# Values and gate columns from seven products a tile pair, dilated values put in slot order through DRAM

## The reference, cut to what matters

```
proj = h @ w_in
q_n, kv_n, gate_n, qkv_d, merge = jnp.split(proj, IN_SPLITS, axis=-1)
...
gate_n = jax.nn.sigmoid(gate_n)                       # 24 columns
kv_n   -> NSA keys and values: compressed, selected, window
qkv_d  -> 3 dilation groups x 4 heads x 64: q, k, v
...
for g, (window, d) in enumerate(DIL_PAIRS):           # d = 1, 4, 16
    # sub(): token t of the sequence goes to subsequence t % d
    o, lse = banded_attention(sub(q[:, :, g]), sub(k[:, :, g]), sub(v[:, :, g]), window // d, ...)
```

## Time and profile before

| | |
|---|---|
| time, median of 3 runs | 1754.91 us (1751.19 to 1756.32) |
| the profiled execution, its own time | 1753.52 us |
| its span (first to last instruction) | 1751.6 us |
| busy: PE, PE weight load, DVE, ACT, POOL | 1628.7, 1069.8, 646.8, 406.9, 176.3 us |
| mean granted TensorE clock | 0.98 of full speed |

### The profile page before, as it was taken

How to read it: one execution, slowest core, us unless ns; L and a number is a source line. 1 busy time by engine, 2 the same in 40 slices (tenths; PEclk the granted TensorE clock), 3 DMA queues, 4 the chain that set the end, 5 groups by cost and what they waited for, 6 DMA issues and landing times. The chain is left out here.

```text
span 1751.6 us, 37114 instructions
## 1 busy us (share of the span) xinstructions
PE 1628.7 (93%) x16025; PEld 1069.8 (61%) x16025; DVE 646.8 (37%) x1594; ACT 406.9 (23%) x908; POOL 176.3 (10%) x220
## 2 busy tenths in 40 slices
PE   5999999999999998999999999999999999998783
PEld 3444445898777786644444445556777767666562
DVE  3533332001767666766655455561000000000003
ACT  4000000001666666610010003221121122111112
POOL 1205000000111110000000000001111111111100
PEclk9999999999999999999999999989999999999996
DMA  9874224131011107334452172169999999999996
GB/s 341 258 230 112 74 84 146 37 104 42 2 44 44 33 2 237 111 111 129 120 145 83 37 280 85 68 258 390 391 383 384 394 387 382 396 392 397 406 385 229
DMA packets 146623, 356.07 MB, mean 203 GB/s; under 512 B 14751, under 2 KB 94231, under 8 KB 121851
## 3 DMA queue, kind: packets, MB, share of 16 engines
q1 hardware_dynamic: 120656, 305.50, 47.0%
q0 software_dynamic: 12656, 28.01, 6.0%
q10 hardware_dynamic: 13148, 20.18, 3.3%
HBM read 320.53 MB, written 45.36 MB: 209 GB/s over the span
## 5 line engine op out<-in xcount | busy, mean ns | idle before, releaser
L2635 PE MATMUL psum<-sb_m_xT,sb_m_ring 128*64 128x64 f32 (+2 forms) x4096 | 152.0, 235 | 22.0 <-issue 17.7
L2635 PEld LDWEIGHTS psum<-sb_m_xT,sb_m_ring 128*64 128x64 f32 x4096 | 147.8, 140 | 35.6 <-issue 34.7
L2384 ACT ACTIVATE sb_m_xT<-psum,sb_rowmod 128x64 f32<-128x64 f32 (+2 forms) x256 | 81.7, 424 | 216.3 <-PE psum L2623 216.3
L2519 DVE TENSOR_TENSOR sb_m_hT<-psum,sb_m_sg 128x256 f32<-128x256 f32 (+2 forms) x32 | 15.3, 477 | 308.9 <-PE psum L2635 308.9
L748 PE MATMUL psum<-sb_vD,sb_room 128*128 128x512 f32 x240 | 104.7, 593 | 0.2 <-DVE sb_vD L685 0.2
L2635 PE MATMUL psum<-sb_m_xT,sb_front 128*64 128x64 f32 (+2 forms) x2560 | 94.5, 236 | 9.9 <-issue 7.3
L2635 PEld LDWEIGHTS psum<-sb_m_xT,sb_front 128*64 128x64 f32 x2560 | 92.4, 142 | 17.2 <-issue 16.9
L1008 ACT ACTIVATE sb_d_probs<-sb_d_probs,sb_d_nmax 128x640 f32<-128x640 f32 (+7 forms) x128 | 92.9, 735 | 1.6 <-DVE sb_d_nmax L1048 1.0
L2642 PE MATMUL psum<-sb_m_ring,sb_m_hT 128*64 128x512 f32 (+2 forms) x256 | 84.5, 611 | 5.6 <-DMA sb_m_ring<-in_exp_w_dram 4.7
L780 PE MATMUL psum<-sb_b_wvd,sb_rows 128*128 128x256 f32 x384 | 88.9, 394 | 0.0
L780 PEld LDWEIGHTS psum<-sb_b_wvd,sb_rows 128*128 128x128 f32 x384 | 84.9, 286 | 3.3
(11 more groups left out here) (384 smaller groups left out, 2408.8 us busy)
## 6 DMA issues: line engine op xcount, KB each, us to landing
sb_m_ring<-in_exp_w_dram SPq DMA_DIRECT2D x48, 2048.0 KB, 34.4
sb_front<-in_exp_w_dram SPq DMA_DIRECT2D x30, 2048.0 KB, 33.8
sb_rows<-in_exp_w_dram SPq DMA_DIRECT2D x18, 2048.0 KB, 36.5
sb_g_ada<-in_ada_w_dram SPq DMA_DIRECT2D x16, 1024.0 KB, 5.3
d_qk<-sb_n_b_sel ACTq DMA_DIRECT2D x20, 512.0 KB, 3.2
sb_front<-in_w_in_dram SPq DMA_DIRECT2D x16, 512.0 KB, 5.4
sb_front<-d_qk SPq DMA_DIRECT2D x15, 512.0 KB, 7.5
sb_n_b_sel<-in_w_in_dram SPq DMA_DIRECT2D x10, 512.0 KB, 8.9
```

What stands on the lines that cost most here:

```text
L2384: last = act.activation(dst[:, kk, 0:w], src, ACT.Identity, scale=k.rowmod[:, 0, kk:kk + 1], bias=k.rowmod[:, 1, kk:kk + 1])
L2635: mm = pe.matmul(k.psum[part, which, c * w:(c + 1) * w], view[:, kk, first:first + 2 * CAPS - 1:2], x[:, kk, 0:w], start=(kk == 0), stop=( ...
```

## The change

The values are now made like queries and keys, by seven products. The second part of `stage_projections` has eight rounds (`v` = 0 to 7). A round takes a pair of token tiles (t and t + 4) and a pair of column blocks: rounds 0 to 3 the NSA values and dilation group 0 (each with 12 of the 24 gate columns, 268 in all), rounds 4 to 7 dilation groups 1 and 2 (256 columns each). The token sums `tok` are those of the first part. The DVE makes four weight sums for each pair of blocks (`v_sums`), ACT copies M1 of each round, and the DVE adds the products up. A round has 7 products of 4 matmuls.

All products now have the tokens in the order of the sequence. The dilated values of all three groups are written by the DVE to staging tiles, stored by SP to a new DRAM tensor `d_v`, and at the end of the stage read back from there by 24 transfers with the step of 4 or 8 tokens on the DRAM side. PE waits for them before the first scores of the dilated stage (`k.s_vd`).

The staging tiles and a weight sum lie in `b_sel[0]`, into which `load_bias` loads. So SP issues `load_bias` when the last store to `d_v` has landed, and the 24 transfers behind it. Keys and queries are loaded after round 4. The compressed hidden layer is made after round 3, its output after round 4.

```diff
-            sp.wait_ge(s_hid, 4)
-            ... (keys and queries)
+            for v in range(NV):
+                for c in (C11, C22, C12, C21):
+                    if set_of(v, c) > 0:
+                        t = v % HT + out_tile[c]
+                        sp.wait_ge(s_vused, vused(v, c))
+                        sp.dma_start(k.d_v[set_of(v, c) - 1, t * P:(t + 1) * P, :], staged[SLOT[c]]
+                                     ).then_inc(s_vst[SLOT[c]], 16)
+                if v == HT:
+                    sp.wait_ge(s_hid, 4)
+                    ... (keys and queries)
+            for c in (C11, C12, C21, C22):
+                sp.wait_ge(s_vst[SLOT[c]], 16 * stores_of(c, NV - 1))
             sp.wait_ge(s_table, 1)
-            sp.wait_ge(s_v, NT)
             ahead.load_bias(sp, k, 0)
+            v0, v1, v2 = (k.d_v[g].rearrange("s (h d) -> s h d", d=DH) for g in range(DIL_G))
+            for t in range(NT):
+                r, b = divmod(t, 2)
+                sp.dma_start(vD[:, 0, t, :, 0:DH], v0[t * P:(t + 1) * P]).then_inc(k.s_vd, 16)
+                sp.dma_start(vD[:, 1, t, :, 0:DH], v1[512 * b + r:512 * b + r + 509:4]).then_inc(k.s_vd, 16)
+                sp.dma_start(vD[:, 2, t, :, 0:DH], v2[t:t + 8 * (P - 1) + 1:8]).then_inc(k.s_vd, 16)
...
-            for n, (s, t) in enumerate(vjobs):
-                if n % 2 == 0:
-                    act.wait_ge(s_v, n + 1)
-                    ...
-                    act.copy(dst, k.psum[:, 4 + (n + 2) % 4, 0:256].rearrange("p (h d) -> p h d", d=DH)).then_inc(s_va, 1)
+            for v in range(NV):
+                n = width[v // HT]
+                act.wait_ge(s_v, vdone(v, M1))
+                if v >= 1:
+                    act.wait_ge(s_vused, vused(v - 1, U2))
+                act.copy(vm1[:, 0:n], k.psum[:, vbank(v, M1), 0:n]).then_inc(s_vm1, 1)
...
+            def v_sums(grp):
+                dve.tensor_tensor(s1s[grp], a21, a22, ALU.add).then_inc(sem, 1)
+                dve.tensor_tensor(s2s[grp], s1s[grp], a11, ALU.subtract).then_inc(sem, 1)
+                dve.tensor_tensor(a21, a11, a21, ALU.subtract).then_inc(sem, 1)
+                dve.tensor_tensor(s4s[grp], a12, s2s[grp], ALU.subtract).then_inc(sem, 1)
...
+            def v_product(v, i, x, w):
+                grp, t = divmod(v, HT)
+                n = 7 * v + i
...
                 if n >= 4:
-                    pe.wait_ge(s_vd if n % 2 else s_va, (n - 4) // 2 + 1)
-                tokens = dilated_tokens(max(s - 1, 0), t)
-                for kk in range(KD):
-                    mm = pe.matmul(k.psum[:, 4 + (n + 2) % 4, 0:rhs.shape[-1]], tokens(hT[:, kk, :]), rhs, ...)
+                    was, j = divmod(n - 4, 7)
+                    pe.wait_ge(s_vm1 if j == M1 else s_vused, was + 1 if j == M1 else vused(was, last_use[j]))
+                for kk in range(HK):
+                    mm = pe.matmul(k.psum[:, vbank(v, i), 0:width[grp]], x[:, kk, t * P:(t + 1) * P], w[:, kk, :], ...)
```

More of the change, by code:

```diff
@@ L182, in __init__ @@
         self.d_qk = dram("d_qk", (R_ALL, S))
+        self.d_v = dram("d_v", (DIL_G, S, DIL_H * DH))
         self.d_dil = dram("d_dil", (DIL_G, S, DIL_H, DH + 2))
@@ L573, in stage_projections, with set_of, stores_of @@
         last_use = {M6: U2, M5: U5, M7: U3, M2: C11, M3: C12, M4: C21}
-        vjobs = [(s, t) for s in range(4) for t in range(NT)]
-        CMP_AT, OUT_AT = 9, 14
+        HT, HK = NT // 2, KD // 2
+        NV = 2 * HT
+        SPLIT = HT - 1
+        flat = spare[:, 0:4, :].rearrange("p a t -> p (a t)")
+        three = lambda at, n: [at[:, HK * n * i:HK * n * (i + 1)].rearrange("p (k c) -> p k c", k=HK) for i in range(3)]
+        vx, vy = [wva, wvd[:, 0]], [wvy, wvd[:, 1]]
+        width = [RV, 256]
+        s1s, s2s, s4s = zip(three(flat, RV), [stage[0].rearrange("p a (k c) -> p (a k) c", k=2),
+                                              stage[1].rearrange("p a (k c) -> p (a k) c", k=2),
+                                              ahead.b_sel[0][0][:, :].rearrange("p (k c) -> p k c", k=HK)])
+        vm1, vu2, vu5 = (g2row[:, RV * i:RV * (i + 1)] for i in range(3))
+        vu3 = ahead.last[:, 0:RV]
+        staged = [ahead.b_sel[0][1][:, 256 * i:256 * (i + 1)] for i in range(4)]
+        SLOT = {C11: 0, C12: 1, C21: 2, C22: 3}
+        out_tile = {C11: 0, C12: HT, C21: 0, C22: HT}
+        def set_of(v, c):
+            return 2 * (v // HT) + (c in (C21, C22))
+        vbank = lambda v, i: 4 + (7 * v + i + 2) % 4
+        vdone = lambda v, i: 7 * v + i + 1
+        vused = lambda v, i: 7 * v + i + 1
+        def stores_of(c, v):
+            return sum(1 for w in range(v + 1) if set_of(w, c) > 0)
         block = k.block(mem)
@@ L731, in _ @@
                                     ).then_inc(s_out, 1)
[L732 to L738, removed]
+                dve.wait_ge(s_v, vdone(v, M3))
+                put(C12, M3, u5_)
+                dve.wait_ge(s_vused, vused(v, U3))
+                dve.wait_ge(s_v, vdone(v, M4))
+                put(C21, M4, u3_)
         @block.tensor
@@ L765, in _ @@
                 product(g, M4, a22, tok[3])
-            for n, (s, t) in enumerate(vjobs):
-                if t == 0:
-                    pe.wait_ge(s_wv[s], 32 if s == 0 else 16)
+            def v_product(v, i, x, w):
+                grp, t = divmod(v, HT)
+                n = 7 * v + i
                 if n == 0:
@@ new lines, in compressed_out @@
+            def compressed_out():
+                pe.wait_ge(s_gelu, 2)
+                for hc in range(2):
+                    mm = pe.matmul(k.psum[0:DH, 0, 0:NSA_KV * NC], w2c[:, 0, hc, :], act1[:, 0, hc, :],
+                                   start=(hc == 0), stop=(hc == 1))
+                mm.then_inc(s_o, 1)
+                pe.wait_ge(s_gelu, 4)
+                for h in range(NSA_KV):
+                    for hc in range(2):
+                        mm = pe.matmul(k.psum[0:NC, 2, h * DH:(h + 1) * DH], act1[:, 1, hc, h * NC:(h + 1) * NC],
+                                       w2c[:, 1, hc, :], start=(hc == 0), stop=(hc == 1))
+                mm.then_inc(s_o, 1)
@@ L820, in __init__ @@
         self.graw = hold.rest[:, 1024:1024 + NT * 3 * NSA_H].rearrange("p (t h) -> p t h", t=NT)
+        self.last = hold.rest[:, 1024 + NT * 3 * NSA_H:]
         self.wq = [self.b_sel[0][x][:, :].rearrange("p (k c) -> p k c", k=KD) for x in range(2)]
```

158 lines of the change are left out of this document (106 added, 52 removed).

## The result

The changed kernel takes 1765.88 us (median of 7 runs, 1759.01 to 1768.63), the kernel before on the same chip 1754.91 (7 runs, 1751.19 to 1757.51). The ratio is 1.0057, with a 95% interval of 1.0044 to 1.0071: on 1755 us that is 10.0 us slower, give or take 2.4. The forecast was 1762, with 1754 to 1773 as its range.

A forecast was written before the change was run, and what follows sets the result against it. PE's own work was taken to bound the value part: 19.8 us saved, 4.8 lost waiting, 1.5 to the clock, then SP's list behind the last product starts NSA 5.9 us later, plus 1 for clock: +6.9, 1762 us, range 1754 to 1773.

The forecast's parts named there:

- Fewer products: Value part on PE: 448 instructions in place of 512, weight loads without a step; 98.9 us, 19.8 us less.
- The wait at the first round: First value round: PE waits at M7 for ACT's copy of M1, queued behind four weight loads; +4.8 us.
- The rounds themselves: Later value rounds: DVE adds, bank reuse and second weight sums stay covered by the products; costed at nothing.
- What SP does behind it: Stage's end: last store, six bias loads, 24 reads of `d_v` hold the barrier; NSA starts at 431.8 us, +5.9.
- NSA stage at a low clock: Start of the NSA stage: the clock is low after 20 us of PE idleness; 1 us added.
- The sum: Whole kernel: NSA start +5.9 us and clock 1 us make +6.9 us, 1762 us on the median.
- only the issue counts: Rival, SP's reads: data keep pace with SP, no clock fall in the first round; +2.4 us, 1757; 25%.
- Slow pieces: Rival, SP's reads: 577 pieces a us, SP ends at 439; +14 us with clock loss, 1769 to 1772; 17%.
- SP is not in the way: Rival, stage's end: reads leave SP faster than any here; if they cost nothing, -7.9 us, 1747; 8%.
- The skill's rule: Reads of `d_v`: below 512 bytes read-modify-write, so 256-byte pieces are no cheaper than 512; about 1770 us.

The follow-up runs named there:

- no_step: Kernel before, with tokens of dilation groups 1 and 2 read side by side, not with a step (outputs differ, whole time not comparable); 1998.32 us, ratio 1.1394.
- reads_later: Changed kernel with SP's 24 reads of `d_v` moved from ahead of the barrier into the NSA stage; 1753.08 us, ratio 0.9984 to the kernel before.
- by_head: Changed kernel with the same 12,288 pieces of 256 bytes read by 16 transfers, four per head, not 24; 1766.03 us, ratio 1.0061 to the kernel before.
- copy_first: Changed kernel with ACT's four compression weight loads issued behind its copy of the first M1; 1758.36 us, ratio 1.0016 to the kernel before.
- bias_early: Changed kernel with reads in the NSA stage, ACT's first M1 copy ahead of its weight loads, bias tables loaded after round 5; 1739.98 us, ratio 0.9908.
- wide_pieces: Changed kernel with each `d_v` row read as one piece of 1024 bytes, not four of 256 (outputs differ, time not comparable); 1965.96 us, ratio 1.1192.
- gap_filled: Changed kernel with five idle products ahead of M7 in the first round, where PE waited for ACT; 1766.87 us, ratio 1.0058 to the kernel before.

## Why the prediction was right, and what in it was off

- **Fewer products:** right. Rounds that nothing holds up take 12.65 us in the first four and 12.09 in the others: 50.6 + 48.4 us, where 98.9 were foreseen. The step of the weight loads as the reason for the slow ones was shown by `no_step`.
- **The wait at the first round:** right in place, releaser and length: at full pace M7 would have followed at 294.62 + 7.2 = 301.8 us, it came at 306.44, 4.6 later against 4.8 foreseen. The clock behind it was mis-sized. I gave the fall of 3 us even odds and put in 1.5; it came, and the three products behind the gap took 8.29 us in place of 5.42, 2.9 us more (1.8 in `reads_later` and `by_head`). `copy_first` gained 7.2 us, about what both together cost.
- **The rounds themselves:** I had the DVE held for 2 us in round 6 and hidden. It was held for 7.8 us by a store of `d_v`, nearly all of it hidden: rounds 4 to 7 took 49.0 us in place of 48.3, of which 0.4 us lie in round 6. With the clock this makes the value part 122.4 us where I had 120.4: 1.9 us of the miss.
- **What SP does behind it:** the step that was right in kind and short in size. Last product to first bias load: 2.5 us (3.5 foreseen). Six bias loads: 3.0 (2.7). The 24 reads: 17.05 (13.8). Barrier: 1.1 (1.3). The tail in all: 23.7, where I had 21.3. The range for the reads, 7.7 to 21.3 us, held; the 13.8 that I took was too low, and so were both estimates behind it. At the steady pace a read took 0.595 us from issue to issue and not the 0.49 of the earlier trace rows, and the pieces ran at 858 to 898 a us and not at 1000. I also had SP 3 to 4 us ahead of the data; in place of that two issues stalled for 2.7 us, right behind the bias loads, which land some 4 to 5 us after their issue. The steady pace (24 x 0.105 = 2.5 us) and the stall are what stands between 17.05 us and the 11.8 by issue alone.
- **NSA stage at a low clock:** I added 1 us. The clock was low for some 8 us of the stage, to about 448.6 us. Before it was low for over 6, and the stage is as long as before (240.1 against 240.4): nothing more is lost there.
- **The sum:** +6.9 foreseen, +10.0 measured: +1.9 in the values, +2.4 in the tail, -1.2 in the NSA stage. The chain of causes and the sign hold. Two terms were too small and one too large, so part of the closeness is luck.
- **The rivals:** "only the issue counts" is out: the reads took 5.3 us more than its 11.8, and the clock did fall. "Slow pieces" at 577 a us is out as a pace, but the time came out between it and the forecast. "SP is not in the way" is out for after; it describes what `bias_early` makes of the change by moving the reads.
- **The skill's rule:** by the Trainium skill ("DMA: Bandwidth & Descriptors", Specifications) transfers below 512 bytes are read, modified and written; the prediction drew from it that a piece of 256 would save nothing against one of 512. These reads into SBUF do not bear that out: 858 to 898 pieces of 256 bytes a us, against 577 of 512. In bytes the smaller are slower all the same, 222 GB/s in `by_head` against 293, as the full rate for 512 bytes and more that the prediction quotes would have it.

Not tried: SP's reads split over a second queue, and the store of whole heads, which would make the pieces longer without touching the layout of `vD`.

## What to carry to other kernels

A stage that ends in a barrier is as long as the longest list, that of the queue that only issues transfers too. Before PE's work is cut short, look at what stands behind the last product on each other engine. Here 19.8 us were saved in products and 21.8 added to the tail, 17.1 of them for reads that nobody needed for another 240 us. When a wait is removed, ask what lands next: the reads moved alone gave 12.8 of 17.1 us, and the bias tables loaded early then gave another 7.9 (ratio 0.9953 to 0.9908). A bank that is reused sooner makes a wait out of whatever an engine has ahead of its first copy.

## What was not expected of the hardware

- In the kernel before, a weight load of 128 x 128 in float32 took 190 ns with its columns side by side and a median of 332 ns where they had a step of 4 or 8, and the instructions of 256 columns behind it started 0.237 us apart in place of 0.2156; without the step (`no_step`) both went back.
- With the bytes of a read unchanged, its issue on SP took longer with more pieces: 0.43 us with 128 (`wide_pieces`), 0.51 to 0.62 with 512 (after), both at the steady pace. The issues of `by_head` with 1024 pieces went from 0.43 us, the first, to 1.58, and in its steady part one line took 0.63 and another 0.86 to 1.02, so pieces are not all that sets it.
- Where PE was kept busy with idle products through a wait (`gap_filled`) the granted clock stayed at 1.00 (2.4 GHz); where it idled 4.16 us the clock was 0.50 (1.2 GHz) from 306 to 312 us in after, and for 3 to 4 us in `by_head` and `reads_later`.
